# Handing the last sum of squares from VectorE to GpSimd and TensorE, and moving one norm's reduction into a product, in a two-model transformer kernel

## What is computed

```python
def rms_norm(x, g):
    xf = x.astype(jnp.float32)
    y = xf * lax.rsqrt(jnp.mean(xf * xf, axis=-1, keepdims=True) + EPS)
    return (y * g.astype(jnp.float32)).astype(x.dtype)
...
        x = x + gm * sq_relu_mlp(modulate(rms_norm(x, g_mlp[l]), sm, cm), w_mlp1[l], w_mlp2[l])
...
    return rms_norm(x, g_final)
...
    proj = x @ w_in          # even_mixer; x is here rms_norm_2(x, mix_norm_g[0])
```

## Time and profile before

| | |
|---|---|
| median of 3 runs | 1644.16 us (1643.83 to 1649.12) |
| the profiled execution's own time | 1644.16 us |
| its span | 1642.4 us |
| TensorE matmul busy | 1566.7 us (95% of the span) |
| VectorE busy | 1033.1 us (63%) |
| ScalarE busy | 748.1 us (46%) |
| GpSimd busy | 104.5 us (6%) |
| mean granted TensorE clock | 0.983 of 2.4 GHz |

### The profile page before, as it was taken

How to read it: one execution, slowest core, us unless ns; L and a number is a source line. 1 busy time by engine, 2 the same in 40 slices (tenths; PEclk the granted TensorE clock), 3 DMA queues, 4 the chain that set the end, 5 groups by cost and what they waited for, 6 DMA issues and landing times.

```text
span 1642.4 us, 27303 instructions
## 1 busy us (share of the span) xinstructions
PE 1566.7 (95%) x11312; PEld 1411.5 (86%) x11312; DVE 1033.1 (63%) x1505; ACT 748.1 (46%) x1066; POOL 104.5 (6%) x105
## 2 busy tenths in 40 slices
PE   4998999999999998989999999999999997999997
PEld 3797686887878786968999989999999997999997
DVE  4744756343343347576665668658786878887785
ACT  4213634222232333164544455666564657565553
POOL 0100000000000000000000010201020100020110
PEclk9999999999999998999999999999999999999999
DMA  9752154243242332325445543235455443545551
GB/s 396 285 233 73 68 214 177 105 147 134 102 153 102 133 148 99 107 77 206 156 169 187 187 172 104 94 130 187 180 180 180 166 169 129 180 180 180 181 183 47
DMA packets 36237, 258.81 MB, mean 158 GB/s; under 512 B 4055, under 2 KB 4056, under 8 KB 5168
## 3 DMA queue, kind: packets, MB, share of 16 engines
q1 hardware_dynamic: 29664, 211.85, 35.8%
q0 software_dynamic: 6480, 45.63, 7.3%
HBM read 256.41 MB, written 1.05 MB: 157 GB/s over the span
## 4 chain that ended last, share of the span: by engine, by line
PE 80%; DVE 12%; ACT 5%; issue 2%; DMA 0%; DVEq 0%; SPq 0%; ACTq 0%
PE ps L486 17%; PE ps L488 16%; PE ps L487 16%; PE ps L506 5%; PE ps L507 5%; PE ps L508 5%; PE ps L559 2%; DVE w_lo L1533 2%; PE ps L561 2%; PE ps L560 2%; PE ps L575 2%; ACT w_hi L1083 1%; DVE small L1662 1%; PE ps L598 1%; DVE wgt L1679 1%
## 5 line engine op out<-in xcount | busy, mean ns | idle before, releaser
L1083 ACT ACTIVATE w_hi<-w_raw 128x1024 fp32r<-128x1024 f32 x380 | 397.6, 1056 | 560.0 <-PE ps L488 337.6
L1533 DVE TENSOR_TENSOR w_lo<-w_raw,w_hi 128x1024 fp32r<-128x1024 f32 x380 | 466.3, 1231 | 233.7 <-ACT w_hi L1083 230.3
L486 PE MATMUL ps<-h_hi,w_hi 128*128 128x256 f32 (+1 forms) x1616 | 501.3, 310 | 6.1 <-DVE h_lo L1585 4.5
L487 PE MATMUL ps<-h_lo,w_hi 128*128 128x256 f32 (+1 forms) x1616 | 496.3, 307 | 0.0
L488 PE MATMUL ps<-h_hi,w_lo 128*128 128x256 f32 (+1 forms) x1616 | 496.2, 307 | 0.0
L486 PEld LDWEIGHTS ps<-h_hi,w_hi 128*128 128x128 f32 x1616 | 310.0, 192 | 29.7 <-issue 11.3
L488 PEld LDWEIGHTS ps<-h_hi,w_lo 128*128 128x128 f32 x1616 | 310.1, 192 | 14.1
L487 PEld LDWEIGHTS ps<-h_lo,w_hi 128*128 128x128 f32 x1616 | 310.2, 192 | 13.2
L486 PE MATMUL ps<-g_hi,w_hi 128*128 128x256 f32 (+1 forms) x448 | 140.4, 313 | 0.0
L506 PE MATMUL ps<-g_hi,w_hi 128*128 128x256 f32 (+1 forms) x448 | 140.4, 313 | 0.0
L507 PE MATMUL ps<-g_lo,w_hi 128*128 128x256 f32 (+1 forms) x448 | 140.4, 313 | 0.0
(11 more groups left out here) (327 smaller groups left out, 2225.9 us busy)
## 6 DMA issues: line engine op xcount, KB each, us to landing
w_raw<-in_w_stream SPq DMA_DIRECT2D x190, 1024.0 KB, 4.8
ada_r<-in_w_ada POOLq DMA_DIRECT2D x20, 1024.0 KB, 5.5
ada_g<-in_w_ada POOLq DMA_DIRECT2D x16, 1024.0 KB, 7.5
ada_r<-in_w_ada SPq DMA_DIRECT2D x4, 1024.0 KB, 15.2
ada_g<-in_w_ada SPq DMA_DIRECT2D x4, 1024.0 KB, 25.1
ada_s<-in_w_ada POOLq DMA_DIRECT2D x4, 1024.0 KB, 5.1
x<-in_x_in SPq DMA_DIRECT2D x2, 1024.0 KB, 6.2
pmat<-in_pool_mats POOLq DMA_DIRECT2D x2, 1024.0 KB, 8.0
```

The costliest lines, as they stand in the source:

```text
L486: mm(o, wh, hi[:, k, cols], start=(k == 0), stop=False)
L487: mm(o, wh, lo[:, k, cols], start=False, stop=False)
L1083: A(w_hi[:, n % 2, k, :].rearrange("p k n -> p (k n)"), w_raw[:, n % 4, k.start * CH:k.stop * CH], ACT.Copy)\
L1533: TT(w_lo[:, n % 2, k, :].rearrange("p k n -> p (k n)"), w_raw[:, n % 4, k.start * CH:k.stop * CH], w_hi[:, n % 2, k, :].rearrange("p k n ...
```

## The change

Five edits, in the words of the code:

1. `norm_sums` of all norms from 1 to 8 takes three parts instead of two: `acc2`, and both halves of step 3's squares. VectorE's addition of the two halves (L1542) and the semaphore `sq_last` are gone; TensorE waits for ScalarE's squares themselves (`sq_done`).
2. For norm 4 VectorE adds nothing any more. The two additions of steps 1 and 2 and the addition of `acc2`'s halves are made by GpSimd.
3. The loads of `wgk` and `wgk2` and the memset of `gkT` stand on GpSimd behind these additions and behind the wait for the last `gated`, where only three memsets stood before.
4. In the last four chunks ScalarE squares first and makes the high part after; VectorE makes the low part of a step behind the `gated` of its own chunk (and the part 1 of its `split_lo`) instead of ahead of the next chunk's `gated`. The split of `wgk` is moved on both engines to where the even mixer's loop begins.
5. TensorE's sums of norm 4 are moved to the middle of EV0 and the broadcast ahead of its eighth feature tile, both ahead of the small product with `wgk`.

```diff
@@ gpsimd
-            pool.wait_ge(g_ready, G0["mlp1"] + 32)
+            for j in (1, 2):
+                pool.wait_ge(sq_done, 16 + j + 1)
+                if j == 2:
+                    pool.wait_ge(sq_used, 13)
+                nc.gpsimd.tensor_tensor(acc2[:, :, :], acc2[:, :, :], sq[:, j % 2, :, :], ALU.add).then_inc(sq_used, 1)
+            pool.wait_ge(sq_used, 14)
+            nc.gpsimd.tensor_tensor(acc2[:, 0, :], acc2[:, 0, :], acc2[:, 1, :], ALU.add).then_inc(sq_used, 1)
+            pool.wait_ge(psum_free, N_EV)
             pool.dma_start(wgk[:, :, :], w_gk).then_inc(gk_in, 16)
             pool.dma_start(wgk2[:, :], w_gk2).then_inc(gk_in, 16)
             pool.memset(gkT[:, :], 1.0).then_inc(gk_ones, 1)
-            pool.wait_ge(psum_free, N_EV)
@@ norm_sums
                 pe.wait_ge(sq_used, 3 * k + 3)
-                if k:
-                    pe.wait_ge(sq_last, k)
-                parts = (acc2[:, 0], sq[:, 1, 0])[:2 if k else 1]
+                pe.wait_ge(sq_done, 4 * k + 4)
+                parts = (acc2[:, 0], sq[:, 1, 0], sq[:, 1, 1])[:3 if k else 1]
@@ tensor, even mixer
-                    gemm_f(n, h_hi, h_lo, slice(0, SEQ), (h_ready, H0["ev"]))
-                    norm_sums(4)
+                    gemm_f(n, h_hi, h_lo, slice(0, SEQ), (h_ready, H0["ev"]), **norm_inside(4))
                     ...
                     last.then_inc(gk_done, 1)
-                    norm_broadcast(4)
@@ scalar, quarter
+                            squares(2 * l + 2, c - 4, n + per * q)
                             if l:
-                                act.wait_ge(psum_free, n + per * q + 1)
                                 raw_hi(4, c - 4)
-                            squares(2 * l + 2, c - 4, n + per * q)
-                            if l and c == 6:
-                                act.wait_ge(gk_in, 32)
-                                A(wgk_hi[:, :, :], wgk[:, :, :], ACT.Copy).then_inc(wgk_hi_ready, 1)
@@ scalar, ahead of the even mixer's loop
+            act.wait_ge(gk_in, 32)
+            A(wgk_hi[:, :, :], wgk[:, :, :], ACT.Copy).then_inc(wgk_hi_ready, 1)
@@ vector, add_squares
+                if j == 3:
+                    return
                 w = NORMS[k][3]
                 dve.wait_ge(sq_done, 4 * k + j + 1)
-                if j == 3:
-                    TT(sq[:, 1, 0, 0:w], sq[:, 1, 0, 0:w], sq[:, 1, 1, 0:w], ALU.add).then_inc(sq_last, 1)
-                    return
@@ vector, quarter
-                            last = it is None and l
-                            if last and 4 < c < 7:
-                                raw_lo(4, c - 5)
-                                if c == 6:
-                                    add_squares(4, 1)
                             gated(n, 2 * (c - 4), l, 40, at)
-                            if last and c == 7:
-                                raw_lo(4, 2)
-                                raw_lo(4, 3)
-                                ...
-                                add_squares(4, 2)
-                                add_squares(4, 3)
                         if it is not None or c < 7:
                             split_lo(m, at if it is not None else same, (1,))
                         ...
+                        if it is None and c >= 4 and l:
+                            raw_lo(4, c - 4)
@@ vector, ahead of the even mixer's loop
+            dve.wait_ge(wgk_hi_ready, 1)
+            TT(wgk_lo[:, :, :], wgk[:, :, :], wgk_hi[:, :, :].bitcast(F32), ALU.subtract).then_inc(wgk_lo_ready, 1)
```

More of the change, by code:

```diff
@@ L235, in build_program @@
         norm_raw, norm_hi, x_final = sem("norm_raw"), sem("norm_hi"), sem("x_final")
-        sq_last = sem("sq_last")
         relu_ready, ghi_ready = sem("relu_ready"), sem("ghi_ready")
@@ L1923, in quarter @@
                         else:
-                            last = it is None and l
-                            if last and 4 < c < 7:
-                                raw_lo(4, c - 5)
-                                if c == 6:
-                                    add_squares(4, 1)
-                            gated(n, 2 * (c - 4), l, 40, at)
-                            if last and c == 7:
-                                raw_lo(4, 2)
-                                raw_lo(4, 3)
-                                dve.wait_ge(wgk_hi_ready, 1)
-                                TT(wgk_lo[:, :, :], wgk[:, :, :], wgk_hi[:, :, :].bitcast(F32), ALU.subtract)\
-                                    .then_inc(wgk_lo_ready, 1)
-                                add_squares(4, 2)
-                                add_squares(4, 3)
+                            gated(n, 2 * (c - 4), l, 40, at)
                         if it is not None or c < 7:
```

## The result

The changed kernel takes 1654.1 us (median of 6 runs, 1652.24 to 1657.36) against 1644.01 (6 runs, 1643.08 to 1649.12): a ratio of 1.0051, with an interval of 1.0037 to 1.0066, or 6 to 11 us slower (it compares more runs than these, 39 of the kernel after; the quotient of the two medians alone would be 1.0061). The forecast was 1645.0 us, with a range up to 1648.5. The profiled execution took 1651.72 us with a span of 1649.5.

A forecast was written before the change was run, and what follows sets the result against it. TensorE, busy for 95% of the span, was taken as the bound. 1644.16 us, plus 1.1 at the joint of the models, minus 0.25 at the other norms, gave 1645.0 us; range for 8 in 10: 1641.8 to 1648.5.

The forecast's parts named there:

- Part A: Last four chunks: the new order removes the PSUM stall, so EV0 starts right behind chunk 87; -1.3 us.
- Part B: Middle of EV0: TensorE idles 1.9 us for GpSimd's additions instead of 0.67 behind EV0; +1.2 us, bounds 0 to +2.0.
- the estimate of 3.4: GpSimd's addition chain ahead of norm 4's sums: 3.4 us from the skill page alone, instead of 4.65 used.
- Part C: Norm 4's sums: the third part brings four products more at 0.22 us; +0.9 us.
- Part D: Norm 4's broadcast: 18 matmuls, 2.16 us, cover a 2.4 us chain, so TensorE waits +0.3 us.
- Part E: Loads of wgk, issued by GpSimd at about 966.3, land before they are wanted; cost 0.
- Part F: Clock behind norm 4's sums: one low stretch again as before, so 0; bounds -1.65 and +3.4 us.
- rival 2: Wait and sums in EV0: the clock stays low for long, beyond 5 us; price +3.4, total 1648.4 us; chance 0.13.
- Part G: The seven other norms: each saves the wait for L1542 and pays 0.22 us a tile; together -0.25 us.
- a tail of the prediction's bounds: Behind norm 6: the low clock, 0.61 over 4.40 us, could go; -1.7 us more, total 1640.5 us.
- The joint's sum: Joint of the models around EV0: -1.3 + 1.2 + 0.9 + 0.3 = +1.1 us, a shift lasting to the end.
- The two signs of being wrong: Idle under 1 us or over 3 in the middle of EV0; a low clock of 10 us behind the sums.

The follow-up runs named there:

- e3: Kernel after with GpSimd's three additions cut to 4 columns each, all waits kept; ratio to the kernel before 1.0007.
- e2: Kernel after with raw_lo of step 2 behind gated of chunk 87 instead of ahead of it; median 1645.54 us, ratio to before 1.0001.
- e7: Kernel before with 60 additions of 1024 elements on GpSimd through layer 1's MLP, on buffers nobody reads; time up 4.6% (1.0430 to 1.0490).
- e4: Kernel before with edit 1 alone: three parts in every norm's sums, no step-3 addition on VectorE; ratio to before 1.0011.
- e1: Kernel after with norm 4's additions made by VectorE again, none by GpSimd; median 1649.34 us, ratio to before 1.0018.
- e10: e6 with edit 5 added: norm 4's sums in the middle of EV0, additions on VectorE; median 1651.53 us, ratio to before 1.0029.
- e5: Kernel after with 40 matmuls of 256 columns, result unread, put ahead of norm 4's waits; ratio to before 1.0047.
- e6: Kernel before with the order of edit 4 alone, additions on VectorE, two parts, sums behind EV0; 1646.33 us, ratio to before 0.9999.
- e9: e6 with three parts in the sums of norms 5 and 6 alone; 1645.49 us, ratio to before 0.9991.

## Why the prediction was wrong

**Part A, right as far as TensorE goes, wrong in what is behind it.** EV0 started 1.4 us sooner (1.3 forecast), but by a hair: `gated` of chunk 86 was to end 1.6 us ahead of EV0 (959.9 and 961.5), and ended 0.1 us ahead (962.82). That it still came in time was luck. "The last `gated` comes at 962.7 (behind `raw_lo` of step 2)" is the step that failed. It took `raw_lo` at 0.88 us and so put GpSimd's effect on VectorE at nothing. On the forecast's time axis, 1.5 us ahead of the trace after, `gated` came at 966.8, 4.1 late: 1.3 from the `raw_lo` of step 1, held by GpSimd's first addition (2.73 us), and 2.8 from that of step 2, held by the second and the third (3.71 us). Without the additions' work (e3) the two `gated` start where the forecast had them, within 0.1 us.

**Part B, the wrong engine and the wrong size.** The idle was 4.79 us, not 1.9. GpSimd itself was quicker than I took it: 2.38 and 1.32 us for 3.0 and 1.5, its chain of 3.8 nearer to the estimate of 3.4 worked out from the Trainium skill (GPSIMD Engine Reference, Elementwise side-by-side) and put aside than to the 4.65 of the sum. The rows could have told it. The means of 1.55 and 1.76 us in the earlier trace rows mix two cases, an instruction that has the way free at 1.3 and one that starts beside a `w_lo` at 1.6 to 2.25; the same lines with their shortest, median and longest, in ns (the kernel before):

```profile
L429 POOL TENSOR_TENSOR x<-x,acc x4: 1270/1768/2248, 1031.7 to 1036.4; 128x512 f32<-128x512 f32 x4
L441 POOL TENSOR_TENSOR ffn_p<-conv_y,gelu_g x18: 1297/1572/1657, 1131.8 to 1601.7; 128x512 f32<-128x512 f32 x18
```

GpSimd's additions ended at 968.14, and with GpSimd alone to wait for the sums would have started at 968.3, as e2 shows with its idle of 2.24. The last to come was ScalarE. The warning in the Trainium skill (GPSIMD Engine Reference, Key points: contention with VectorE instructions of two SBUF inputs) was the rule that decided, and I had used it in one direction only, as a price on GpSimd. The trace agrees with it in the other: 0.88 to 3.71 us here, 1.23 to 3.19 in e7, and 0.47 unchanged for `gated`, which has one operand in PSUM.

The kernel before had shown it, too, in rows that the argument left out. GpSimd multiplies from 1031.73 on, and a pair of `w_lo`, twice 1.23 us elsewhere, takes 4.19; and another single one takes 1.54:

```profile
1031.73 6.95 POOL L429 TENSOR_TENSOR x<-x,acc 128x512 f32<-128x512 f32 x4 [53.27 <-ACT attnX L1335]
```

```profile
1033.36 4.19 DVE L1533 TENSOR_TENSOR w_lo<-w_raw,w_hi 128x1024 fp32r<-128x1024 f32 x2 [2.50 <-ACT w_hi L1083]
...
1338.03 1.54 DVE L1533 TENSOR_TENSOR w_lo<-w_raw,w_hi 128x1024 fp32r<-128x1024 f32 x1 [1.65 <-ACT w_hi L1083]
```

(The last stands in the trace at the odd mixer, beside GpSimd's `xr_lo`.) I had read L441's 1.55 us against L433's 1.04 as GpSimd's loss, though L441 takes 1.3 with the way free, and not asked what VectorE paid.

**Part C, right.** 24 rows instead of 16; e4 confirms the 0.9 and what it saves.

**Part D, hidden.** The 18 matmuls took 4.0 us at the low clock, longer than the chain to the diagonal, so there was no wait.

**Part E, right.** The loads of `wgk` were issued at 969.5, and no engine waited for them.

**Part F, on its upper bound.** The low clock lasted 10.2 us: rival 2, with its +3.4, came in with 0.13. Counted in the trace, the low clock cost the sums 2.0 us (4.71 for 24 rows of 0.111), the rest of EV0 and the broadcast 2.7 (6.53 for 24 matmuls of 0.12 and 0.92), and gave back 1.5 at the product with `wgk` (2.73 instead of 4.25): +3.2. The two misses may not be independent, as the prediction treated them: the low stretch is 10.2 us behind an idle of 4.79 in both traces of after, 6.8 behind 1.44 and 2.24 (e1, e2), 3.4 behind 0.81 (e3). But e10 has 3.4 behind 2.88, and e5 6.8 with no idle, so that a longer wait brings a longer low clock is likely and not shown.

**Part G, right in direction.** Norms 5 and 6 lost their 0.96 us, and no low clock came behind norm 6 (the window of the earlier trace rows in the trace after, 8.2 us later and so at the same place behind the sums):

```profile
1334.60:1339.00 4.40, 4.40 (x36) 4.35 (x36) 3.49 (x5) 3.54 (x7) 0.00 (x0) 1.00 0.41 128
```

That was a tail of the prediction's bounds (-1.7), and it is the rule here: all nine traces with three parts at norm 6 have no low stretch there, and all four with two parts (before, e6, e7, e10) have one of 3.4 us. No ratio shows the gain, and behind norm 3 a low stretch comes rather more often with three parts (6 of 8 traces, against 1 of 4 with two, e7's load left out), so what the three parts are worth over the whole is open.

The joint's sum, measured: -1.4 (A) + 4.3 (idle 4.95 from pitch to pitch, for 0.67) + 0.9 (C) + 3.2 (clock) = +7.0; forecast was +1.1. The two signs of being wrong that the prediction had named came both, an idle of over 3 us and a low clock of 10. The 0.88 us taken for `raw_lo` explains the excess of the idle (e2 and e3); the low clock came behind it. What is left between the joint's 7.0 and the 8.4 of the ratio lies inside the ratio's interval.

## What to carry to other kernels

Moving an elementwise operation to an idle GpSimd isn't free for VectorE: price it by asking which VectorE instructions with two SBUF operands will start while it runs, count each as held until it ends (as every one looked at here was), and then follow what stands behind them in VectorE's order. Where such a move is wanted, put beside it a VectorE instruction with a PSUM operand (`gated` was at 0.47 us throughout), or one that nobody waits for. And a reduction that sits in the middle of a product for its latency needs its inputs ready by then: here 4.3 us more of waiting there were followed by 3.2 us more from the clock.

## What the runs showed of the hardware that was not expected

- Additions of 1024 elements on GpSimd, 60 in a row, and VectorE's two-operand instructions alternate one by one: 3.03 us for 2.4 on GpSimd, 3.19 for 1.23 and 2.84 for 0.69 on VectorE, 76 us in all.
- TensorE's clock fell to 1.2 GHz behind or within runs of one-column products without any idle ahead of them: in e5, with 4.8 us of dense matmuls ahead, 1.4 us after they began, for 6.9 us; with 24 rows and no idle (e4) for 3.4 us. With 16 rows behind a dense stretch and no idle (e6, e9) it stayed at 1.00. Each is one trace.
- GpSimd's memsets, which read nothing, did not hold VectorE's `raw_lo` (0.88 us, the kernel after at 971.11).
- Runs of one kernel scatter by up to 9 us (1641.8 to 1650.9 for the kernel before, 35 runs), more than the joint's whole gain in e6. The joint of the kernel after repeats from trace to trace within 0.8 us (45.97 and 45.23).
